# A one-core fp32 transformer pair: the attention layers' last group reordered, the experts' selections moved behind later units, and x's norm sums moved behind the first unit's parts

## The reference, cut to what matters

```python
def first_block(x, ...):
    for i in range(2):                         # DEPTH
        h = rmsnorm(x, attn_norm[i]); proj = h @ w_in[i]
        ...                                    # rope; 8 dilated heads, 8 windowed heads
        mix = concatenate([rmsnorm(merge_heads(oa), mix_norm_a[i]),
                           rmsnorm(merge_heads(ob), mix_norm_b[i])])
        x = x + mix @ w_out[i]
        h = rmsnorm(x, ffn_norm[i])
        if i % 2 == 0: x = x + swiglu(h, dense_w_gate, dense_w_up, dense_w_down)   # D_FF 3584
        else:          x = x + moe_swiglu(h, router, moe_w_gate, moe_w_up, moe_w_down)  # 8 experts, top 2
    return rmsnorm(x, final_norm)
# second model: modulated ffn halves of context and x, a token mixer (Hyena convolution
# and differential attention), and a last ffn half
ctx = ffn_half(ctx, ...); x = ffn_half(x, ...)
```

## Time and profile before

| what | us |
|---|---|
| median of 3 runs | 2653.58 (2653.3 to 2659.06) |
| the profiled execution's own time | 2659.7 |
| its span, first to last instruction | 2657.9 |
| PE busy | 2548.6 (96% of the span) |
| DVE busy | 1814.3 (68%) |
| ACT busy | 1452.1 (55%) |
| POOL busy | 54.4 (2%) |
| mean clock granted to PE, share of full | 0.978 |

### The profile page before, as it was taken

The page is one execution under the profiler, slowest core; times in us unless marked ns, Lnnn a source line. Parts: engine busy times, 40 slices in busy tenths (PEclk is TensorE's granted clock), DMA queues, the critical chain, the costliest instruction groups (busy, mean ns, idle before and its releaser), DMA issues.

```text
span 2657.9 us, 33567 instructions
## 1 busy us (share of the span) xinstructions
PE 2548.6 (96%) x11951; PEld 2023.4 (76%) x11951; DVE 1814.3 (68%) x1779; ACT 1452.1 (55%) x1613; POOL 54.4 (2%) x40
## 2 busy tenths in 40 slices
PE   7899999889999999999999998999999999998998
PEld 6578887667878788888878786888884688776787
DVE  6464446558898888888888985645444475776544
ACT  4454444547777777776767774435432343465443
POOL 0000000010000000000000000500000000000000
PEclk9899999889999999999999999999999999998999
DMA  6865552659999999999999995755544244435551
GB/s 216 297 207 189 189 174 90 243 174 374 351 353 348 354 342 347 356 351 342 360 328 372 327 341 203 227 191 183 187 145 130 85 143 131 129 107 173 193 185 68
DMA packets 327743, 631.65 MB, mean 238 GB/s; under 512 B 14089, under 2 KB 112937, under 8 KB 327465
## 3 DMA queue, kind: packets, MB, share of 16 engines
q1 hardware_dynamic: 326792, 627.35, 68.0%
q0 software_dynamic: 864, 3.15, 0.4%
HBM read 629.40 MB, written 1.05 MB: 237 GB/s over the span
## 4 chain that ended last, share of the span: by engine, by line
PE 85%; DVE 7%; ACT 4%; issue 3%; DMA 1%; SPq 0%; DVEq 0%; ACTq 0%
PE ps L829 19%; PE ps L903 19%; PE ps L933 11%; PE ps L858 10%; PE ps L1303 6%; PE ps L763 5%; PE ps L1330 2%; PE ps L1235 1%; DVE As L2290 1%; PE ps L1038 1%; PE ps L958 1%; PE ps L918 1%; PE ps L842 1%; ACT Bs L1724 1%; ACT As L1694 1%
## 5 line engine op out<-in xcount | busy, mean ns | idle before, releaser
L2290 DVE TENSOR_TENSOR As<-ringA,As 128x2048 fp32r<-128x2048 f32 x318 | 730.9, 2300 | 227.4 <-ACT As L1613 131.9
L903 PE MATMUL ps<-As,xgs 128*128 128x512 f32 x2688 | 660.7, 395 | 5.7 <-DVE As L2290 3.0
L903 PEld LDWEIGHTS ps<-As,xgs 128*128 128x128 f32 x2688 | 494.8, 188 | 112.3 <-issue 5.8
L1694 ACT ACTIVATE As<-ringA 128x2048 fp32r<-128x2048 f32 x224 | 428.8, 1914 | 28.3 <-PE ps L903 28.1
L829 PE MATMUL ps<-As,xs 128*128 128x512 f32 x1456 | 376.1, 396 | 3.9 <-DVE hh L2325 3.9
L933 PE MATMUL ps<-Bs,hds 128*128 128x512 f32 x1332 | 322.4, 391 | 11.8 <-DVE hds L2351 9.0
L829 PEld LDWEIGHTS ps<-As,xs 128*128 128x128 f32 x1456 | 271.9, 189 | 63.3 <-DVE hh L2325 4.8
L933 PEld LDWEIGHTS ps<-Bs,hds 128*128 128x128 f32 x1332 | 248.6, 188 | 69.9 <-issue 16.5
L2370 DVE TENSOR_TENSOR Bs<-ringB,Bs 128x2048 fp32r<-128x2048 f32 x111 | 254.1, 2290 | 12.4 <-ACT Bs L1724 10.8
L858 PE MATMUL ps<-Bs,hds 128*128 128x512 f32 x1056 | 250.6, 393 | 4.1 <-issue 4.1
L1724 ACT ACTIVATE Bs<-ringB 128x2048 fp32r<-128x2048 f32 x111 | 213.1, 1920 | 69.4 <-PE ps L933 69.4
(11 more groups left out here) (390 smaller groups left out, 3300.3 us busy)
## 6 DMA issues: line engine op xcount, KB each, us to landing
ringA<-in_moe_w_gate SPq DMA_DIRECT2D x112, 1024.0 KB, 5.2
ringA<-in_moe_w_up SPq DMA_DIRECT2D x112, 1024.0 KB, 5.6
ringB<-in_moe_w_down SPq DMA_DIRECT2D x112, 1024.0 KB, 5.6
ringA<-in_w_ff_in SPq DMA_DIRECT2D x132, 512.0 KB, 4.7
ringA<-in_w_in SPq DMA_DIRECT2D x56, 1024.0 KB, 5.3
ringA<-in_w_ada SPq DMA_DIRECT2D x36, 1024.0 KB, 5.8
ringB<-in_w_ff_out SPq DMA_DIRECT2D x33, 1024.0 KB, 5.0
ringA<-in_dense_w_gate SPq DMA_DIRECT2D x28, 512.0 KB, 3.6
```

Source lines behind the costliest of these rows:

```text
L903: m = mm(ps[:, bank, :], lhs(l, tt, k), As[:, h, r, k % 4, :], start=k == 0 and n == 0, stop=k == KC - 1 and n == 2)
L1694: A(As[:, h, 0, :, :], ringA[:, (p["a"] + u) % 2, 4 * h:4 * h + 4, :], ACT.Copy).then_inc(A_high, 1)
L2290: V.tensor_tensor(As[:, h, 1, :, :], ringA[:, (p["a"] + u) % 2, 4 * h:4 * h + 4, :], f32(As[:, h, 0, :, :]), ALU.subtract).then_inc(A_spli ...
```

## The change

No instruction is added or removed on PE; ACT and DVE keep their work, and DVE's expert loop is written out one pair of units further (the loop starts at pair 3 and not at 2), which adds code and no work.

1. Attention, last group of either layer. PE: `values(3)` and `mods(8)` come ahead of the first turn of the mix rows. ACT: the sums of the lower half go ahead of `mods(6)` in group 2, the square root of them behind the last copies of `PT`, with its table loaded ahead behind the first copy of group 3; behind it come the first half of the first out weights, the sums of the upper half, `mods(8)`, their square root, the lower rows' high parts, `spreads(8)` and only then the other half of those weights. DVE: the lower half's scaling goes from group 2 to behind group 3's copies, and the lower rows' low parts go behind the upper half's scaling.
2. Experts, DVE: the second `add` goes behind the `part_low` of unit 4, the selection for the way back behind unit 4 and the next expert's selection behind unit 5 (all were behind unit 3).
3. Context's first block: a hook `within(n)` behind `hidden`; the sums of x's norm (ACT) and the scaling (DVE) go there, behind unit 1's `hidden`.

```diff
@@ PE, heads(l), g == 3
+                        values(g)
+                        mods(8)
                         pe.wait_ge(nm_ready, 4 * (l + 1))
                         for tt in range(TILES):
                             turn_rows(f"mix{l}", tt, 0)
-                        values(g)
-                        mods(8)
                         spreads(8)
@@ ACT, layer l
                         if j == 0:
+                            if g == 3:
+                                nc.scalar.preload_act_table(ACT.Sqrt)
                             spreads(2 * g + 1)
+                    if g == 2:
+                        for tt in range(TILES):
+                            tile_stats(f"mix{l}", tt, O, [(o_done, 4 * l + 2)], slice(0, D // 2), tt)
                     if g < 3:
                         mods(2 * g + 2)
...
                         mods(2 * g + 3)
-                    if g == 2:
-                        for tt in range(TILES):
-                            tile_stats(f"mix{l}", tt, O, [(o_done, 4 * l + 2)], slice(0, D // 2), tt)
-                        tile_root(0, 2, D // 2)
+                tile_root(0, 2, D // 2)
...
+                weight_high(p, 0, 0)
+                for tt in range(TILES):
+                    tile_stats(mix, tt, O, [(o_done, 4 * (l + 1))], slice(D // 2, D), 2 + tt)
+                mods(8)
+                tile_root(2, 4, D // 2)
                 for tt in range(TILES):
                     rows_high(mix, tt, 0, mixc)
-                for h in range(2):
-                    weight_high(p, 0, h)
-                mods(8)
-                for tt in range(TILES):
-                    tile_stats(mix, tt, O, [(o_done, 4 * (l + 1))], slice(D // 2, D), 2 + tt)
-                tile_root(2, 4, D // 2)
                 spreads(8)
+                weight_high(p, 0, 1)
                 for tt in range(TILES):
                     rows_high(mix, tt, 1, mixc)
@@ DVE, layer l, g == 3 and behind it
                         for tt in range(TILES):
-                            rows_low(mix, tt, 0, mixc)
+                            tile_scale(mix, tt, O, 1, lower, tt)
                     outputs(g)
-                    if g == 2:
-                        for tt in range(TILES):
-                            tile_scale(mix, tt, O, 1, lower, tt)
                 weight_low(p, 0, 0)
                 for tt in range(TILES):
                     tile_scale(mix, tt, O, 2, upper, 2 + tt)
+                for tt in range(TILES):
+                    rows_low(mix, tt, 0, mixc)
                 weight_low(p, 0, 1)
@@ DVE, expert(e)
-                    if n in (2, 3) and not first:
-                        add(e - 1, n - 2)
-                    if n == 3:
+                    if n == 2 and not first:
+                        add(e - 1, 0)
+                    if n == 4:
                         if not first:
                             dve.wait_ge(selg_tp, e)
                         one_hot(e, 2 * e + 2, True)
-                        if not final:
-                            dve.wait_ge(gathered, 2 * e + 2)
-                            one_hot(e + 1, 2 * e + 3, False)
+                    if n == 5 and not final:
+                        dve.wait_ge(gathered, 2 * e + 2)
+                        one_hot(e + 1, 2 * e + 3, False)
...
                         part_low(e, i - 1, u, 1)
+                    if isinstance(i, int) and i == 2 and u == 0 and not first:
+                        add(e - 1, 1)
...
-                blocks(dve, NB1, body, 2)
+                blocks(dve, NB1, body, 3)
@@ feed, on ACT and on DVE, behind hidden(...)
+                    if within and isinstance(i, int):
+                        within(2 * i + u)
@@ ACT: from x_rows(1) to x_stats(1), called by within
-                        tile_stats("ff0x", tt, x, [(x_ready, XR["final"])])
-                        tile_root(tt, tt + 1, D, 1e-6)
-                    nc.scalar.preload_act_table(ACT.Silu)
@@ DVE: from x_rows(0) to x_scale(1), called by within
-                    dve.wait_ge(x_ready, XR["final"])
-                        tile_scale("ff0x", tt, x, tt + 1)
```

More of the change, by code:

```diff
@@ L2295, in x_parts, with feed @@
                     x_low(src, done, h, high, split)
[L2297 removed]
+            def feed(p, T, e=0, ahead=False, head=1, leads=True, drains=True, after=None, within=None, split_rows=None, settles=True):
                 nb = p["nb"]
@@ L2808, in context_end @@
                     scaled("mixc", cs)
-            feed(ph["ff0c"], 2, ahead=True, head=2, drains=False, after=x_rows)
+            feed(ph["ff0c"], 2, ahead=True, head=2, drains=False, after=x_rows, within=x_scale)
             feed(ph["ff0x"], 2, head=2, leads=False, after=context_end)
```

20 lines of the change are left out of this document (15 added, 5 removed).

## The result

The changed kernel takes 2634.85 us (median of 5 runs, 2627.88 to 2638.85), the kernel before, run beside it, 2657.95 (median of 5): ratio 0.9914, 95% interval 0.9900 to 0.9929, 22.9 us less (18.9 to 26.6). Run a second time in another batch of runs (the last experiment) the ratio was 0.9893, 0.9877 to 0.9909. The forecast was 2634.0 in 2625 to 2645. The profiled execution took 2632.58 us, its span is 2630.8.

A forecast was written before the change was run, and what follows sets the result against it. PE bounds the kernel, through its idle time and half-rate clock. Terms 6 + 7 + 6.3 + 5.2 = 24.5 us off the profiled 2659.7 give 2635.2; 19.5 off the median 2653.58 gives 2634, range 2625 to 2645.

The forecast's parts named there:

- Layer 0: Last attention group: PE's waits of 2.38 and 0.88 go; gain 5.0 us without the clock, 6.4 with it, taken as 6.
- T: End of the last attention group's value products; in layer 0 to come 4.96 us earlier, 6.4 with the clock.
- the landmark: Second half of the out projection's first tile, 13th product; in layer 0 forecast at T + 10.5, with a 1.3 us wait.
- Layer 1: Same attention pieces: 4.3 us if half rate stays, 10.3 at full rate from the first turn; taken as 7.
- Experts: DVE's low hidden half of unit 4 starts sooner: 1.0 us for each of experts 1 to 6, 0.3 for expert 0; 6.3.
- Context's block: Context's first block: the 4.07 us wait goes, a new one of 1.5 comes; gain 5.2, 3 with half rate remaining.
- The median: Earlier median 2653.58 us, 6.1 below the profiled run; some 5 us of clock terms assumed already in it, giving 2634.
- The rule against it: Table load plus drain, some 2.66 us: second weight copy 1.38 later, PE waits some 0.4 per layer, sum 23.7; not adopted.
- Only the idle time comes back: Rival: half rate stays wherever it is; 18.6 us from the profiled run, 2635 to 2641 us; chance 0.2.
- The stalls only move: Rival: selections return in units 5 and 6, first out product waits 3 us more; gain 13, 2643 us; chance 0.1.
- No net change: Rival: PE gives its gain back at the next transfer or router step; 2649 to 2657 us; chance 0.07.
- Slower by the clock: Rival: half-rate stretches grow in both layers and the context's block, costing 18.5 against 13 gained; 2659 us; chance 0.03.

The follow-up runs named there:

- 1: The kernel before with the attention part of the change alone; ratio to the kernel before 0.9954 (0.9941 to 0.9967).
- Experiment 10: The changed kernel with both selections behind unit 4, the next expert's one unit sooner; ratio to the kernel before 0.9917 (0.9902 to 0.9931).
- experiment 12: The changed kernel run again unaltered, for a second draw of the clock; ratio to the kernel before 0.9893 (0.9877 to 0.9909).
- experiment 4: The kernel before with only DVE's expert loop written out one pair of units further; ratio to the kernel before 1.0005 (0.9995 to 1.0014).
- experiment 9: The changed kernel without the early load of the root's table; ratio to the kernel before 0.9911 (0.9895 to 0.9927).
- Experiment 5: The kernel before with the attention's new order on PE alone, ACT and DVE as before; ratio to the kernel before 1.0033 (1.0022 to 1.0044).
- experiment 6: The kernel before with the attention's new order on ACT and DVE alone, PE as before; ratio to the kernel before 0.9972 (0.9961 to 0.9983).
- experiment 11: The changed kernel with the lower sums ahead of the last group's first copy of turned weights; ratio to the kernel before 0.9934 (0.9922 to 0.9947).

## Why the prediction was right, point by point

- **Layer 0 (6; came 6.8, 7.5 over more profiles).** The mean of the four profiles with the whole new attention order unaltered (changed, 1, 10, 12) is 29.4 us, of the four with the old one 36.9. The waits ahead of the turns went and the sums cost nothing in their gap, as the working had it. But two terms were off and offset each other, so that the 6 came out is in part luck. T came 8.4 us ahead, counted from the stretch's start, and not 5.0 to 6.4: the half rate on `mods(6)`, which stands ahead of the first windows of the earlier trace rows and which the working did not price, went too (1.92 us for 3.41). And the landmark is at T + 11.8 and not at T + 10.5: the working let the loads "land ahead of need", and the first weights land 2.2 us after ACT could take them, so PE waits 2.2 us in three places and not 1.3 in one. In experiment 12 the half rate on `mods(6)` is back, T comes 6.8 ahead and the landmark is at T + 10.8. The clock gave 3.7 of the 6.8, where the sum had at most 1.4.
- **Layer 1 (7; came 8.8, and 6.8 by the means of 17.6 and 24.4).** The high end, 10.3, was worked out for the full rate throughout and has the mechanism right: its landmark is at T + 10.6, and it stands at T + 10.7 (525.71 behind 515.05). PE's own work up to it is 8.2 us and not 9.2, so PE waits 0.47 + 1.95 there. Half rate is left for 3.4 of 16.9 us, which takes 1.7 from 10.3 and gives 8.6. The 7 was a choice between two ends and not a sum; that the mean over four profiles comes so near to it says that the clock there differs from draw to draw.
- **Experts (6.3; came 7.5).** The mechanism is shown: `hds` of unit 4 ahead of the addition, no wait. In experts 1 to 6 it gives 1.1 us each (forecast 1.0), in expert 0 0.6 (0.3) and in expert 7 0.25 (nothing). The step that was mis-sized is "so 0.3 to 0.4 comes back" in unit 5: 0.2 came back. I subtracted 0.61 for a `hds` that the row has as 0.42, and 0.84 for a selection that takes 0.79; with 0.42 the slack is 0.9 and one selection just fits. Experiment 10 puts 0.66 more there and gets a wait of 0.58. The longer head costs nothing (experiment 4).
- **Context's block (5.2; came 5.7, and 4.8 by the means of 41.5 with the part and 46.3 without it).** The new wait of 1.5 came as 1.40. The clock was 1.00 with the part in six profiles of seven with the hook in its place.
- **The median.** I took 5 us of clock as already in the median of 2653.58. Beside the changed kernel the kernel before had 2657.95, so most of that was chance of three runs. The forecast time of 2634 holds all the same, since the gain in the runs, 22.9, lies between my 19.5 and 24.5; the second batch's 28.4 lies above both. That the time came within 1 us is luck, as the changed kernel's medians in its two batches differ by 6.
- **The rule against it.** After the load at 123.79 the next instruction starts at 125.08, 1.29 later, and the copy behind it at 125.16; in experiment 9 the load takes the same and the time of the kernel does not move. Of the 24 loads in the changed kernel's profile 16 have the next instruction 1.29 us behind their start, and behind the other eight it waits for another engine or a transfer. The Trainium skill (ScalarE: Activation LUTs, What ACT_TABLE_LOAD costs) adds a drain of about 1380 ns. By that rule the second copy would have come at 126.5; the trace has no drain, and PE did not wait.
- **The rivals.** *Only the idle time comes back* is refuted: idle time is 13.7 of 28.8, and over all runs the clock's loss fell from 57 us to 42 and 35. *The stalls only move* is refuted for the experts and true in small for the attention, where DVE's chain gives part of it back in the first product. *No net change* is refuted by the ratio: the code between layer 1's stretch and the experts takes 52.7 us for 52.8, so nothing gave the gain back there. *Slower by the clock* is refuted for this order. Experiment 5 is slower (1.0033), but by a wait for a copy that no rival had, at a clock over its runs as before.
- **What would show it.** Half-rate work in the stretches of the earlier trace rows was to fall under 15 us: in the three stretches that hold them it fell from some 48 us of half-rate time to 7 (twice the shortfall of PEclk times the length). The wait in the product, unit 4's order and the context's wait came as said; the wait in unit 5 came at 0.1, too short to be printed.

That less idle time in the attention stretches goes with a higher clock is shown over whole sets of runs: the attention part alone takes 13.6 us from the clock's loss, its ACT and DVE half 9.1 (experiment 6), and experiment 11 puts two waits of 0.8 to 0.9 us back and has a larger loss than the three kernels with the new order beside it. The single stretches are less sure. In the profiles new against old order gives 0.94 against 0.73 to 0.81 (layer 0), but in layer 1 the old order had 0.53 to 0.76 and the new one 0.90 and 0.74 (experiments 12 and 10). Which wait costs how much clock stays open.

## What to carry to other kernels

Read PE's idle time and its clock as one cost: here 13.7 us of idle time taken away came with 15.1 us of clock, where work had stood at half rate next to the stalls. Compare two kernels between the same counted instructions of the engine that bounds them, several profiles of each, since totals of single executions mix in the clock of everything else; and split every run's span by its mean granted clock, which shows without a profile whether waits or the clock moved. And when the order of one engine moves, move the copies that it waits for as well: PE's new order alone cost 9 us, in waits.

## What the runs showed of the hardware that was not expected

- The granted clock of the same code varies between executions: layer 1's stretch with the old order took 21.30 to 25.66 us (PEclk 0.76 to 0.53), with the new one 16.87 to 19.77 (0.90 to 0.74).
- Waits of 0.7 to 0.9 us on PE, in two kernels, went with 3 to 6 us longer stretches; in one of them the clock was lower over all six runs (0.982 for 0.984 to 0.987 beside it).
- An activation table load of 1.28 us costs just that on ACT: the next instruction starts 1.29 us behind the load's start in all 16 places of the profile where it waits for no other engine.
